# Query projection and product-key scores interleaved head by head, ahead of and between the first expert gathers

## The chip, the cores and the metric

The kernel runs on one core of one Trainium2 chip. The metric is the device time of one launch in microseconds (us); lower is better. The numbers of the kernel before are the median of three runs and one profiled execution.

## The reference, cut to what matters

The program is a two-block transformer on 256 tokens of width 1024, all in float32. The change lies in the first block's product-key expert layer (PEER): queries for 8 heads of 256 columns, each half scored against 128 sub-keys, the best 16 of the 16 x 16 sums chosen, and for each token and head 16 expert rows of `u` and of `v` fetched from a table in HBM.

```python
q = (x @ w_query)                      # 8 heads x 2 halves x 128
s = jnp.einsum('thpd,hpkd->thpk', q, subkeys)
sv, si = lax.top_k(s, 16)
cand = sv[..., 0, :, None] + sv[..., 1, None, :]
top_s, pos = lax.top_k(cand.reshape(..., 256), 16)
gate = softmax(top_s)
act = gelu(einsum('thkd,td->thk', u_tab[expert], x))
out = einsum('thk,thkd->td', gate * act, v_tab[expert])
```

## The kernel before, in words

**Engines and jobs.** The five engines run hand-written streams joined by semaphores. Each PSUM bank use is a job of the list `PLAN` (L34); job j uses bank j modulo 8, TensorE (PE) counts finished jobs in `pe_done`, and whoever copies a bank out counts `evac_done`, in the order of the list.

**Weights.** Query weights come in eight pieces of 1 MB, one for each head (pieces 0 to 7). ScalarE (ACT) casts a piece to a rounded float32r part (`split`, the "hi" part, L433), VectorE (DVE) or GpSimd (POOL) subtracts to get the "lo" part (`split_lo`, L440; L588), and PE forms the product with three matmuls per chunk (L2063 to L2065). Pieces 0 to 3 have raw, hi and lo slots 0 to 3 of their own. Pieces 4 to 7 use hi and lo slots 2, 3, 2, 3, so their cast waits until PE has used the piece two before. Their raw data (`QUERY_RAW`, L390) goes to: piece 4 a part of `PROJ`; piece 5 `SCR[:, 0:2048]`, where the sub-keys lay; piece 6 and 7 the hi and lo slot of piece 1, so that SP loads them only when PE has used piece 1 (L509 to L511).

**Queries and scores.** PE computes `queries(1)`, the rest of head 0, `queries(2)`, a part of the scores of head 0, then `queries(3)` to `(7)`, and then all scores in seven jobs of four matmuls (L2305 to L2333). Transposed queries of all heads lie in `qT`, all of `A`. ACT copies them there (`query_cols`, L921) and the scores into `SCORE` (L981).

**Expert rows.** A unit is one head for one 128-token half: 16 units in all. A unit has 16 gathers (POOL, L637) of one 1 MB buffer each (128 tokens x 2048 floats, `u` and `v` rows together), 256 in all, into 16 buffers `pair_buf` (L294). For each buffer DVE takes the dot product of the `u` part with the token (L1645), ACT makes gelu, the weight and a diagonal matrix for each block of four (L938, L943, L952), and PE sums the `v` part with it: eight matmuls for each block (`sum_rows`, L2347), then `rows_summed` is counted up and POOL may refill the four buffers. One full-float32 matmul stands as two instructions in the rows.

**The first unit.** Its buffers still hold weights, so `first_pairs` (L647) waits before the gathers: 0 to 3 (raw slots) for the splits of pieces 0 to 3, 4 and 5 (hi and lo slot 0) for the use of piece 0, 6 and 7 for the splits of pieces 6 and 7, 8 (`SCR`) for the split of piece 5, 9 and 10 (hi and lo slot 2) for the use of piece 6, 11 and 12 (slot 3) for the use of piece 7, 13 and 14 (`A`) and 15 (`B`, the sub-keys) for the last scores. POOL issues in program order, so whatever stands behind a waiting gather waits with it; the gathers of unit 1 follow (`pairs`, L663), each block of four when PE has summed the block of unit 0 (`rows_summed`), and when DVE has the indices of the unit (`idx_ready`).

**Route stages.** DVE's top-k of one unit is 17 small stages (L1567 to L1624); the gather indices are ready at stage 13.

Of the kernel before, what the change touches and what calls it, by code (L numbers as in the profile page):

```python
# [14 lines left out]
P = 128  # L15
# [65 lines left out]
def query_job(m):  # L81

    return J[f"query_{m}"] if m < 3 else J["query_rest"] + m - 3


def score_job(m):

    return J["score"] if m == 0 else J["score_rest"] + m - 1
# [52 lines left out]
def build(nc, a, out, at):  # L141
    ctx = ExitStack()
    with ctx:
# [123 lines left out]
        qT = A[:, :].rearrange("p (u t) -> p u t", u=16)  # L267
        SKN = SCR[:, 0:2048].rearrange("p (u n) -> p u n", u=16)
        SKT = B[:, 0:2048].rearrange("p (u n) -> p u n", u=16)
        SCORE = PROJ[:, 0:4096]  # L270
        N2W = PROJ[:, 4096:5120]
# [115 lines left out]
        class Piece:  # L387
# [3 lines left out]
                     RING + 3: ROWS[:, 5 * HALF:6 * HALF], RING + 4: ROWS[:, 9 * HALF:10 * HALF]}  # L391
        pieces, holder, raw_holder, uses, dmas = {}, [None] * 5, [None] * 9, [0] * 5, [0] * 9
        for name, n, h, src in PIECES:
# [5 lines left out]
            if r > RING:  # L399
                w.raw = QUERY_RAW[r]  # L400
            uses[h] += 1
# [53 lines left out]
        def _(sp):  # L455
# [50 lines left out]
            load("query", 4)  # L506
            sp.wait_ge(pe_done, END["subk_rest"])
            load("query", 5)
            sp.wait_ge(*pieces["query", 1].used)  # L509
            for n in range(6, 8):  # L510
                load("query", n)  # L511
# [68 lines left out]
        def _(pool):  # L580
# [66 lines left out]
            def first_pairs():  # L647

                pool.wait_ge(sem("idx_ready"), 1)
                for n in range(TOPK):  # L650
                    if n < 4:
                        query_split(n)
                    elif n == 4:
                        pool.wait_ge(*pieces["query", 0].used)
                    elif n in (6, 7, 8):
                        query_split((6, 7, 5)[n - 6])
                    elif n in (9, 11):
                        pool.wait_ge(*pieces["query", 6 if n == 9 else 7].used)
                    elif n == 13:
                        pool.wait_ge(pe_done, END["score_rest"])  # L660
                    gather(pair_buf[n], a["peer_uv"], 0, n, pair_loaded[n])
# [68 lines left out]
        def _(act):  # L730
# [190 lines left out]
            def query_cols(m):  # L921
# [3 lines left out]
                if m == 0:  # L925
                    d, src = qT[:, 0:2, P:S], PS[:, j % 8, 2 * P:4 * P]
                else:
                    d, src = qT[:, 2 * m:2 * m + 2, :], PS[:, j % 8, :]
                act.copy(d, src.rearrange("p (c t) -> p c t", c=2)).then_inc(evac_done, 1)

# [35 lines left out]
            gate_exp(0)  # L966
            query_cols(1)
            query_cols(0)
            for n in range(4, 8):
                split("query", n)  # L970
                query_cols(n - 2)
            weights(0, 0, 0)
            diag(0, 0, wait=False)
            query_cols(6)
            gate_exp(1)
            query_cols(7)
            for m in range(1, 8):
                j = score_job(m)
                act.wait_ge(pe_done, j + 1)
                act.wait_ge(evac_done, j)  # L980
                act.copy(SCORE[:, m * BANK:(m + 1) * BANK], PS[:, j % 8, :]).then_inc(evac_done, 1)  # L981
# [216 lines left out]
        def _(v):  # L1198
# [352 lines left out]
            nc.vector.tensor_copy(qT[:, 0:2, 0:P], first[:, 2 * P:4 * P].rearrange("p (c t) -> p c t", c=2)).then_inc(sem("head_ready"), 1)  # L1551
# [121 lines left out]
            split_lo(v, "query", 3)  # L1673
            j = J["score"]
            v.wait_ge(evac_done, j)
            freed(nc.vector.tensor_copy(SCORE[:, 2 * P:BANK], bank(j)[:, 2 * P:]), j, wait=True)
            for n in range(4, 6):
                split_lo(v, "query", n)
            v.wait_ge(sem("tokens_scaled"), 1)
            first_dots(0)  # L1680
            for n in range(6, 8):
                split_lo(v, "query", n)
            route_stages(1, 1, range(14))
            first_dots(1)
            route_stages(1, 1, range(14, 17))
            for b in range(2, 4):
                first_dots(b)
            v.wait_ge(evac_done, END["score_rest"])
# [990 lines left out]
```

## Time and profile before

| | |
|---|---|
| median of 3 runs | 1542.4 us (1539.7 to 1542.81) |
| profiled execution, first to last instruction | 1536.3 us |
| mean granted TensorE clock | 0.973 |
| expert rows, software queue q0 | 268.45 MB, 42.1% of 16 engines' span |
| gathers | 256, about 168 us to 821 us of the span |

No time of its own stands for the profiled execution beside its span; the median of the runs lies 6.1 us above the span. In the slices of the profile each digit is a tenth of busy time in one fortieth of the span (38.4 us). GB/s is what all DMA engines of the core moved.

### The profile page before, as it was taken

What the parts mean: (1) busy time and instruction counts of PE and PEld (TensorE: products, weight loads), DVE (VectorE), ACT (ScalarE), POOL (GpSimd) and SP (SyncE); (2) the same over time, 40 slices, a digit from 0 to 9 for tenths busy, and PEclk for the clock granted to TensorE, in tenths of its full rate; (3) what the DMA queues carried; (4) which work ended last, traced back from release to release, by engine and by line L of the source; (5) the groups of instructions that cost most, each with busy time, mean ns of one, the idle gap of its engine ahead of it and who ended that gap; (6) DMA issues with size and microseconds to landing.
All of it is one profiled execution on the core that took longest, in us unless ns stands there. A gap on an engine that the chain in (4) does not pass through costs nothing.

```text
span 1536.3 us, 18265 instructions
## 1 busy us (share of the span) xinstructions
PE 1381.1 (90%) x6001; PEld 969.0 (63%) x6001; DVE 1029.5 (67%) x1917; ACT 710.5 (46%) x1377; POOL 568.9 (37%) x541
## 2 busy tenths in 40 slices
PE   7999998778777887777779999999999999999998
PEld 6887963323333333333336878788888778888887
DVE  4885787666666666666655548659863686498734
ACT  5545453222333332233324463477645655776534
POOL 3040454333333333333344422055433512364414
PEclk9999999998998999999899999999999999999999
DMA  9295699999999999999998510567665443476650
GB/s 315 91 179 189 247 385 422 421 421 422 422 421 422 420 423 422 421 422 422 422 421 312 192 48 13 165 184 203 191 216 194 158 140 92 134 207 195 214 188 28
DMA packets 180739, 414.99 MB, mean 270 GB/s; under 512 B 9178, under 2 KB 113218, under 8 KB 148418
## 3 DMA queue, kind: packets, MB, share of 16 engines
q0 software_dynamic: 37440, 268.45, 42.1%
q1 hardware_dynamic: 143090, 145.66, 30.9%
q8 instruction: 38, 0.62, 0.2%
q14 instruction: 27, 0.22, 0.0%
q10 hardware_dynamic: 144, 0.04, 0.0%
HBM read 409.93 MB, written 4.19 MB: 270 GB/s over the span
## 4 chain that ended last, share of the span: by engine, by line
PE 52%; DMA 23%; DVE 9%; ACT 6%; POOL 5%; issue 4%; ACTq 0%; POOLq 0%; DVEq 0%
DMA expert_rows<-in_peer_uv,route_idx 13%; PE ps L2522 10%; DMA work_b<-in_peer_uv,route_idx 9%; PE ps L2347 8%; PE ps L2063 8%; PE ps L2065 8%; PE ps L2064 8%; PE ps L2523 5%; POOL weights_lo L588 2%; POOL expert_rows L637 2%; ACT weights_hi L433 2%; DVE weights_lo L440 2%; PE ps L2028 1%; DVE expert_rows L1645 1%; POOL ple_proj_lo L588 1%
## 5 line engine op out<-in xcount | busy, mean ns | idle before, releaser
L1645 DVE CUSTOM_DVE_ANT_0 expert_rows<-expert_rows,ps 128x1024 f32<-128x1024 f32 x180 | 219.4, 1220 | 133.9 <-DMA expert_rows<-in_peer_uv,route_idx 132.0
L2347 PE MATMUL ps<-expert_rows,proj 128*128 128x512 f32 x512 | 248.6, 644 | 63.5 <-ACT proj L952 63.5
L637 POOL DMA_INDIRECT expert_rows<-in_peer_uv,route_idx x191 | 184.5, 966 | 288.9 <-PE ps L2347 218.9
L588 POOL TENSOR_TENSOR weights_lo<-weights_raw,weights_hi 128x512 fp32r<-128x512 f32 x116 | 153.4, 1356 | 352.2 <-ACT weights_hi L433 310.3
L433 ACT CAST weights_hi<-weights_raw 128x2048 fp32r<-128x2048 f32 x98 | 185.5, 1917 | 106.3 <-PE ps L2065 82.6
L2347 PEld LDWEIGHTS ps<-expert_rows,proj 128*128 128x128 f32 x512 | 102.9, 206 | 208.4 <-issue 122.5
L2522 PE MATMUL ps<-x_normT,weights_hi 128*128 128x512 f32 x640 | 222.5, 393 | 0.0
L440 DVE TENSOR_TENSOR weights_lo<-weights_raw,weights_hi 128x2048 fp32r<-128x2048 f32 x69 | 163.1, 2370 | 61.2 <-ACT weights_hi L433 60.8
L938 ACT ACTIVATE proj<-proj 128x4 f32<-128x4 f32 x64 | 13.1, 205 | 408.0 <-DVE proj L1645 408.0
L2063 PE MATMUL ps<-weights_hi,x_normT 128*128 128x512 f32 (+1 forms) x496 | 188.2, 379 | 9.3 <-DVE weights_lo L440 3.2
L2065 PE MATMUL ps<-weights_hi,x_normT 128*128 128x512 f32 (+1 forms) x496 | 184.7, 372 | 0.0
L2064 PE MATMUL ps<-weights_lo,x_normT 128*128 128x512 f32 (+1 forms) x496 | 184.6, 372 | 0.0
L2523 PE MATMUL ps<-x_normT,weights_lo 128*128 128x256 f32 x640 | 178.3, 279 | 0.0
L2347 PE MATMUL ps<-expert_rows,scratch 128*128 128x512 f32 x252 | 120.8, 625 | 27.2 <-ACT scratch L952 27.2
L2522 PEld LDWEIGHTS ps<-x_normT,weights_hi 128*128 128x128 f32 x640 | 119.9, 187 | 27.1
L2523 PEld LDWEIGHTS ps<-x_normT,weights_lo 128*128 128x128 f32 x640 | 120.5, 188 | 0.0
L2063 PEld LDWEIGHTS ps<-weights_hi,x_normT 128*128 128x128 f32 x496 | 93.4, 188 | 30.3 <-issue 3.4
L2347 PEld LDWEIGHTS ps<-expert_rows,scratch 128*128 128x128 f32 x252 | 49.5, 201 | 97.8 <-issue 59.0
L2065 PEld LDWEIGHTS ps<-weights_hi,x_normT 128*128 128x128 f32 x496 | 93.4, 188 | 16.6
L2064 PEld LDWEIGHTS ps<-weights_lo,x_normT 128*128 128x128 f32 x496 | 93.5, 189 | 15.6 <-issue 0.2
L1875 DVE SCALAR_TENSOR_TENSOR work_a<-ps,conv_cols,work_a 128x254 f32<-128x254 f32 (+1 forms) x176 | 76.5, 475 | 29.3 <-ACT work_a L1088 25.1
L705 POOL TENSOR_TENSOR hidden_hi<-work_a 128x256 f32 (+1 forms) x44 | 41.8, 950 | 100.3 <-ACT work_a L1068 100.1
(369 smaller groups left out, 2411.3 us busy)
## 6 DMA issues: line engine op xcount, KB each, us to landing
weights_raw<-in_ffn_up SPq DMA_DIRECT2D x88, 512.0 KB, 5.0
weights_raw<-in_ffn_down SPq DMA_DIRECT2D x22, 1024.0 KB, 5.0
weights_raw<-in_ab_w_in SPq DMA_DIRECT2D x14, 1024.0 KB, 5.1
weights_raw<-in_w_in SPq DMA_DIRECT2D x12, 1024.0 KB, 7.9
weights_raw<-in_ple_gate SPq DMA_DIRECT2D x8, 1024.0 KB, 6.3
weights_raw<-in_c_w_in SPq DMA_DIRECT2D x6, 1024.0 KB, 5.7
weights_raw<-in_w_out SPq DMA_DIRECT2D x4, 1024.0 KB, 12.0
weights_raw<-in_peer_w_query SPq DMA_DIRECT2D x4, 1024.0 KB, 11.9
```

Source lines behind the costliest of these rows:

```text
L433: copy(w.hi[:, :], w.raw[:, :]).then_inc(hi_ready[w.h], 1)
L440: eng.tensor_tensor(w.lo[:, :], w.raw[:, :], w.hi[:, :].bitcast(F32), ALU.subtract).then_inc(lo_ready[w.h], 1)
L588: ins = pool.tensor_tensor(w.lo[:, c], w.raw[:, c], w.hi[:, c].bitcast(F32), ALU.subtract)
L637: nc.gpsimd.indirect_dma_start(out=dst, out_offset=None, in_=table, in_offset=bass.IndirectOffsetOnAxis(ap=r_idx[:, q, n:n + 1], axis=0)). ...
L1645: ins = nc.vector.tensor_tensor_reduce(out=rows, in0=rows, in1=tokens, scale=1.0, scalar=0.0, op0=ALU.mult, op1=ALU.add, accum_out=r_dot[: ...
L1875: ins = nc.vector.scalar_tensor_tensor(out=d, in0=PS[:, (j0 + 2 * q + g) % 8, 0:S - n], scalar=CONV[:, l, bass.ds(i * RING + (tap * 2 * FT ...
L2063: pe.matmul(o, x[0], w[0], start=first, stop=False)
L2064: pe.matmul(o, x[0], w[1], start=False, stop=False)
L2065: return pe.matmul(o, x[1], w[0], start=False, stop=last)
L2347: ins = pe.matmul(PS[:, (J[f"peer_{t}"] + m) % 8, :], DIAG[b][:, k, :], rows[:, m * BANK:(m + 1) * BANK], start=False, stop=False, skip_gr ...
L2522: pe.matmul(b.rearrange("p (a t) -> p a t", a=2), hi[:, c, g, :], x_both(c), start=c == 0, stop=False)
L2523: ins = pe.matmul(b[:, 0:S], lo[:, c, g, :], XHI[:, c, :], start=False, stop=c == KC - 1)
```

## The change

- `qT` is a ring of two heads in `SCR[:, 2048:3072]` (0.5 MB) in the place of all of `A`; the raw data of pieces 6 and 7 goes to the two halves of `A`, and the lo parts of pieces 5, 6 and 7 are written over their raw data.
- SP asks for pieces 4, 6 and 7 together behind the sub-keys, then for 5 once the sub-keys are used.
- The score jobs are now one for each head (both halves of tokens), each right behind the queries of the next head; `queries(7)` and the scores of heads 6 and 7 stand behind the first block of expert sums of unit 0.
- The first unit's gathers go in the order 0 to 7, 12, 10, 8, 9, 13, 11, 14, 15 with new waits.
- ACT's and DVE's work is put in a matching order.

```diff
-        ("query_1", 1), ("query_0", 1), ("query_2", 1), ("score", 1), ("query_rest", 5), ("score_rest", 7),
+        ("query_1", 1), ("query_0", 1), ("query_2", 1), ("score_1", 1), ("score_0", 1), ("query_3", 1), ("score_2", 1),
+        ("query_4", 1), ("score_3", 1), ("query_5", 1), ("score_4", 1), ("query_6", 1), ("score_5", 1), ("query_7", 1),
+        ("score_6", 1), ("score_7", 1),
...
-        qT = A[:, :].rearrange("p (u t) -> p u t", u=16)
+        qT = SCR[:, 2048:3072].rearrange("p (s q t) -> p s q t", s=2, q=2)
...
+        SCORE_HEADS = SCORE.rearrange("p (t n) -> p t n", t=TT)
...
-                     RING + 3: ROWS[:, 5 * HALF:6 * HALF], RING + 4: ROWS[:, 9 * HALF:10 * HALF]}
+                     RING + 3: A[:, 0:HALF], RING + 4: A[:, HALF:2 * HALF]}
+        QUERY_LO = {RING + 2: place("query_lo_5", [P, HALF], O_SCR, F32R),
+                    RING + 3: place("query_lo_6", [P, HALF], O_A, F32R),
+                    RING + 4: place("query_lo_7", [P, HALF], O_A + HALF, F32R)}
...
+                w.lo = QUERY_LO[r] if r in QUERY_LO else w.lo
...
-            load("query", 4)
+            for n in (4, 6, 7):
+                load("query", n)
             sp.wait_ge(pe_done, END["subk_rest"])
             load("query", 5)
-            sp.wait_ge(*pieces["query", 1].used)
-            for n in range(6, 8):
-                load("query", n)
...
-                for n in range(TOPK):
+                last_use = {4: 0, 12: 3, 10: 4, 8: 5, 9: 6, 11: 7}
+                for n in (0, 1, 2, 3, 4, 5, 6, 7, 12, 10, 8, 9, 13, 11, 14, 15):
                     if n < 4:
                         query_split(n)
-                    elif n == 4:
-                        pool.wait_ge(*pieces["query", 0].used)
-                    elif n in (6, 7, 8):
-                        query_split((6, 7, 5)[n - 6])
-                    elif n in (9, 11):
-                        pool.wait_ge(*pieces["query", 6 if n == 9 else 7].used)
-                    elif n == 13:
-                        pool.wait_ge(pe_done, END["score_rest"])
+                    elif n in last_use:
+                        pool.wait_ge(*pieces["query", last_use[n]].used)
+                    elif n == 15:
+                        pool.wait_ge(pe_done, END["score_7"])
                     gather(pair_buf[n], a["peer_uv"], 0, n, pair_loaded[n])
 
             def pairs(u, q, blocks=4):
...
+                    d, src = qT[:, m % 2], PS[:, j % 8, :]
...
+            def score_cols(m):
+                j = score_job(m)
+                act.wait_ge(pe_done, j + 1)
+                act.wait_ge(evac_done, j)
+                t0 = 0 if m else 1
+                act.copy(SCORE_HEADS[:, t0:TT, 2 * m * P:2 * (m + 1) * P],
+                         PS[:, j % 8, 2 * P * t0:].rearrange("p (t n) -> p t n", n=2 * P)).then_inc(evac_done, 1)
...
+            act.wait_ge(sem("bias_written"), 16)
             query_cols(1)
             query_cols(0)
-            for n in range(4, 8):
+            split("query", 4)
+            act.wait_ge(pe_done, END["score_0"])
+            query_cols(2)
+            act.wait_ge(lo_ready[pieces["query", 4].h], pieces["query", 4].count)
+            score_cols(1)
+            score_cols(0)
+            for n in (5, 6):
                 split("query", n)
                 query_cols(n - 2)
+                score_cols(n - 3)
             weights(0, 0, 0)
             diag(0, 0, wait=False)
-            query_cols(6)
+            split("query", 7)
+            for m in (5, 6):
+                query_cols(m)
+                score_cols(m - 1)
             gate_exp(1)
             query_cols(7)
-            for m in range(1, 8):
-                j = score_job(m)
-                act.wait_ge(pe_done, j + 1)
-                act.wait_ge(evac_done, j)
-                act.copy(SCORE[:, m * BANK:(m + 1) * BANK], PS[:, j % 8, :]).then_inc(evac_done, 1)
+            score_cols(6)
+            score_cols(7)
...
-            split_lo(v, "query", 3)
-            j = J["score"]
-            v.wait_ge(evac_done, j)
-            freed(nc.vector.tensor_copy(SCORE[:, 2 * P:BANK], bank(j)[:, 2 * P:]), j, wait=True)
-            for n in range(4, 6):
+            for n in (3, 4):
                 split_lo(v, "query", n)
+            v.wait_ge(evac_done, END["score_1"])
+            route_stages(1, 1, range(4))
+            split_lo(v, "query", 5)
             v.wait_ge(sem("tokens_scaled"), 1)
             first_dots(0)
-            for n in range(6, 8):
-                split_lo(v, "query", n)
-            route_stages(1, 1, range(14))
-            first_dots(1)
-            route_stages(1, 1, range(14, 17))
-            for b in range(2, 4):
+            split_lo(v, "query", 6)
+            route_stages(1, 1, range(4, 9))
+            split_lo(v, "query", 7)
+            route_stages(1, 1, range(9, 17))
+            for b in range(1, 4):
                 first_dots(b)
-            v.wait_ge(evac_done, END["score_rest"])
+            v.wait_ge(evac_done, END["score_7"])
...
-                t, h0 = m // 4, (m % 4) * 2
-                pe.wait_ge(evac_done, query_job(h0 + 1) + 1)
+                pe.wait_ge(evac_done, query_job(m) + 1)
                 b = bank(score_job(m))
-                for n in range(0 if m else 2, 4):
-                    u = 2 * h0 + n
-                    ins = pe.matmul(b[:, n * P:(n + 1) * P], qT[:, u, t * P:(t + 1) * P], SKT[:, u, :], start=True, stop=True)
+                for t in range(0 if m else 1, TT):
+                    for q in range(2):
+                        o = (2 * t + q) * P
+                        ins = pe.matmul(b[:, o:o + P], qT[:, m % 2, q, t * P:(t + 1) * P], SKT[:, 2 * m + q, :],
+                                        start=True, stop=True)
                 ins.then_inc(pe_done, 1)
 
             queries(1)
             head_columns(1, J["query_0"]).then_inc(pe_done, 1)
             queries(2)
+            scores(1)
             scores(0)
-            for m in range(3, 8):
+            for m in range(3, 7):
                 queries(m)
-            for m in range(1, 8):
-                scores(m)
-
-            def sum_rows(u, t, last=False):
-
-                for b in range(3 if last else 4):
+                scores(m - 1)
+
+            def sum_rows(u, t, last=False, blocks=range(4)):
+
+                for b in range(3) if last else blocks:
                     if last and b == 2:
                         for _ in range(4):
                             for acc in accs:
@@ -2352,8 +2369,13 @@
                 accs = [bank(J[f"peer_{t}"] + m) for m in range(2)]
                 for acc in accs:
                     pe.matmul(acc, zeros, C[:, 0:BANK], start=True, stop=False, skip_group_check=True)
-                for u in range(0 if t else 2):
-                    sum_rows(u, t)
+                if t == 0:
+                    sum_rows(0, 0, blocks=range(1))
+                    queries(7)
+                    scores(6)
+                    scores(7)
+                    sum_rows(0, 0, blocks=range(1, 4))
+                    sum_rows(1, 0)
```

## Rows read from the trace of the kernel before

**Rows 1.** The profile's slices: DMA busy tenths and GB/s, forty slices.

```profile
DMA  9295699999999999999998510567665443476650
GB/s 315 91 179 189 247 385 422 421 421 422 422 421 422 420 423 422 421 422 422 422 421 312 192 48 13 165 184 203 191 216 194 158 140 92 134 207 195 214 188 28
```

**Rows 2.** Busy time by stretch; columns: engines, granted clock, DMA share, GB/s.

```profile
166.00:190.00 24.00, 24.00 (x203) 24.00 (x202) 15.96 (x20) 8.12 (x8) 6.75 (x6) 1.00 0.90 350
190.00:200.00 10.00, 10.00 (x85) 10.00 (x85) 7.39 (x27) 7.76 (x14) 4.62 (x5) 1.00 0.61 208
200.00:210.00 10.00, 10.00 (x77) 8.80 (x76) 9.76 (x23) 6.24 (x11) 4.37 (x5) 1.00 1.00 410
210.00:217.00 7.00, 7.00 (x18) 3.17 (x17) 4.22 (x7) 4.61 (x18) 2.44 (x2) 1.00 1.00 420
400.00:600.00 200.00, 159.61 (x333) 65.85 (x333) 136.51 (x347) 60.58 (x195) 75.83 (x80) 0.93 1.01 422
```

**Rows 3.** POOL in order of time: start, length, what, idle before and releaser.

```profile
167.82 1.11 POOL L637 DMA_INDIRECT expert_rows<-in_peer_uv,route_idx  x1 [4.38 <-DVE route_idx L1611]
...
190.67 0.94 POOL L637 DMA_INDIRECT expert_rows<-in_peer_uv,route_idx  x1 [14.57 <-DVE weights_lo L440]
195.40 0.94 POOL L637 DMA_INDIRECT expert_rows<-in_peer_uv,route_idx  x1 [3.80 <-DVE weights_lo L440]
196.65 0.94 POOL L637 DMA_INDIRECT scratch<-in_peer_uv,route_idx  x1 [0.30 <-issue]
...
217.37 0.94 POOL L637 DMA_INDIRECT expert_rows<-in_peer_uv,route_idx  x1 [4.62 <-PE ps L2347]
```

**Rows 4.** PE in order of time: the score jobs, zero fill and sums.

```profile
172.36 0.61 PE L2323 MATMUL ps<-work_b,work_a 128*128 128x128 f32 x4
...
207.85 1.88 PE L2354 MATMUL ps<-consts 128*128 128x512 f32 x4
209.57 13.90 PE L2347 MATMUL ps<-expert_rows,proj 128*128 128x512 f32 x32
```

**Rows 5.** The chain that ended last, about 200 us: start, length, what.

```profile
201.76 6.27 PE ps L2323 x56
208.03 0.26 issue
208.28 0.94 POOL work_a L637
```

**Rows 6.** ACT in order of time.

```profile
184.57 1.91 ACT L433 CAST weights_hi<-expert_rows 128x2048 fp32r<-128x2048 f32 x1 [3.38 <-PE ps L2065]
...
190.33 1.90 ACT L433 CAST weights_hi<-expert_rows 128x2048 fp32r<-128x2048 f32 x1 [3.37 <-PE ps L2065]
192.14 0.58 ACT L929 COPY work_a<-ps 128x512 f32<-128x512 f32 x1
192.73 1.28 ACT L938 ACT_TABLE_LOAD   x1
194.03 0.21 ACT L938 ACTIVATE proj<-proj 128x4 f32<-128x4 f32 x1
194.32 0.85 ACT L943 ACTIVATE proj<-proj 128x1 f32<-128x1 f32 x4
195.21 1.28 ACT L952 ACTIVATE proj<-consts,proj 128x128 f32<-128x128 f32 x4
```

**Rows 7.** DVE in order of time: a split, a dot, the last dot of unit 0.

```profile
192.33 2.29 DVE L440 TENSOR_TENSOR weights_lo<-expert_rows,weights_hi 128x2048 fp32r<-128x2048 f32 x1 [2.44 <-ACT weights_hi L433]
...
223.21 1.23 DVE L1645 CUSTOM_DVE_ANT_0 work_b<-work_b,x_norm 128x1024 f32<-128x1024 f32 x1 [1.25 <-DMA work_b<-in_peer_uv,route_idx]
```

**Rows 8.** SP in order of time: query pieces 4, 5, then 6 and 7.

```profile
134.28 6.07 SPq L465 DMA_DIRECT2D proj<-in_peer_w_query  x1
157.41 0.37 SPq L465 DMA_DIRECT2D scratch<-in_peer_w_query  x1
166.57 0.99 SPq L465 DMA_DIRECT2D expert_rows<-in_peer_w_query  x2
```

**Rows 9.** Busy time by stretch, columns as rows 2.

```profile
130.00:146.00 16.00, 16.00 (x76) 13.32 (x76) 5.02 (x8) 5.21 (x16) 0.00 (x0) 1.00 0.95 295
146.00:150.00 4.00, 4.00 (x21) 3.28 (x20) 3.36 (x7) 4.00 (x4) 0.02 (x1) 1.00 0.01 5
150.00:157.00 7.00, 6.36 (x52) 5.73 (x51) 4.25 (x13) 5.90 (x17) 7.00 (x5) 1.00 0.00 0
```

**Rows 10.** Half-microsecond stretches round the lone gather, columns as rows 2.

```profile
191.50:192.00 0.50, 0.50 (x7) 0.50 (x6) 0.00 (x0) 0.50 (x1) 0.10 (x1) 1.00 0.00 0
192.00:192.50 0.50, 0.50 (x7) 0.50 (x6) 0.17 (x1) 0.50 (x2) 0.00 (x0) 1.00 0.99 197
...
195.50:196.00 0.50, 0.50 (x7) 0.50 (x6) 0.50 (x5) 0.50 (x3) 0.50 (x1) 1.00 0.21 66
```

**Rows 11.** The clock after a wait of PE: stretches, columns as rows 2.

```profile
236.00:240.00 4.00, 1.20 (x3) 0.19 (x1) 4.00 (x10) 2.14 (x9) 1.92 (x3) 0.97 1.01 422
240.00:244.00 4.00, 3.76 (x6) 1.73 (x7) 3.04 (x7) 0.19 (x1) 1.84 (x2) 0.61 1.01 420
```

More of the change, by code:

```diff
@@ L81, in query_job @@
 def query_job(m):
-    return J[f"query_{m}"] if m < 3 else J["query_rest"] + m - 3
+    return J[f"query_{m}"]
 def score_job(m):
-    return J["score"] if m == 0 else J["score_rest"] + m - 1
+    return J[f"score_{m}"]
 def shape_constants():
@@ L925, in query_cols @@
                 if m == 0:
-                    d, src = qT[:, 0:2, P:S], PS[:, j % 8, 2 * P:4 * P]
+                    d, src = qT[:, 0, :, P:S], PS[:, j % 8, 2 * P:4 * P]
                 else:
-                    d, src = qT[:, 2 * m:2 * m + 2, :], PS[:, j % 8, :]
+                    d, src = qT[:, m % 2], PS[:, j % 8, :]
                 act.copy(d, src.rearrange("p (c t) -> p c t", c=2)).then_inc(evac_done, 1)
+            def score_cols(m):
[5 more added lines that the diff above has]
+                         PS[:, j % 8, 2 * P * t0:].rearrange("p (t n) -> p t n", n=2 * P)).then_inc(evac_done, 1)
             def gate_exp(u):
@@ L1550, in _ @@
             v.wait_ge(sem("head_turned"), 1)
-            nc.vector.tensor_copy(qT[:, 0:2, 0:P], first[:, 2 * P:4 * P].rearrange("p (c t) -> p c t", c=2)).then_inc(sem("head_ready"), 1)
+            nc.vector.tensor_copy(qT[:, 0, :, 0:P], first[:, 2 * P:4 * P].rearrange("p (c t) -> p c t", c=2)).then_inc(sem("head_ready"), 1)
             norm_lo(1, 1)
@@ L2298, in _ @@
             for u in range(2):
-                ins = pe.matmul(b[:, u * P:(u + 1) * P], qT[:, u, 0:P], SKT[:, u, :], start=True, stop=True)
+                ins = pe.matmul(b[:, u * P:(u + 1) * P], qT[:, 0, u, 0:P], SKT[:, u, :], start=True, stop=True)
             ins.then_inc(pe_done, 1)
```

## The prediction

> **What bounds the kernel here.** I read the slices first: from about 190 us to 820 us DMA moves 420 to 424 GB/s in nearly every slice, and before that it has holes [rows 1]. That is the expert stage. In stretches, 400 to 600 us shows a DMA share of 1.01 while PE is busy 160 of 200 us and DVE 137 [rows 2]: the stage is a stream of 256 gathers of 1.049 MB, and at 422 GB/s one costs g = 1.049 MB / 422 GB/s = 2.485 us. Whatever leaves DMA idle between the first gather (167.82 us [rows 3]) and the last moves the end of the stream one for one, and the rest of the kernel behind it. So the question is only when the 16 gathers of unit 0 are done by DMA, and whether the stream stays full after that.
>
> Where is DMA not full before? 166 to 190 us runs at 350 GB/s on average, which includes 2.1 MB of query pieces 6 and 7, asked for at 166.57 us [rows 2, 8]; 190 to 200 us moves 208 GB/s [rows 2]. The cause stands in POOL's rows: gather 6 waits 14.57 us for a lo split and goes out at 190.67, gather 7 waits again and goes at 195.40, then 8 and the others follow 1.25 us apart [rows 3], faster than DMA takes them. From 200 us DMA is full (410, then 420 GB/s [rows 2]). So two things are to be had: the 2.1 MB in the stream (5.0 us) and the holes round 190 and 196 us.
>
> **PE's stream** is the clock of everything that frees a buffer. ACT's casts of pieces 6 and 7 start when PE is through with pieces 4 and 5, at 184.57 and 190.33: one query piece costs PE 5.76 us [rows 6]. A score job of four matmuls (eight instructions) costs 8 x 6.27/56 = 0.90 us, and POOL's gather 13 goes 0.26 us behind the last [rows 5]. The zero fill costs 209.57 - 207.85 = 1.72 us, one block of sums 13.90/2 = 6.95 us [rows 4].
>
> **Part 1: pieces 6 and 7 loaded early.** DMA is full to 146 us (295 GB/s on average) and empty to 157 us [rows 9]. Two more MB behind piece 4 (asked at 134.28) take 2.1 MB / 295 GB/s = 7.1 us, to about 153 us, ahead of piece 5's request at 157.41 [rows 8]. They stand behind the sub-keys on SP, and SP's long issue (6.07 us for piece 4) delays nothing else, as its next order is piece 5. Cost 0; without that empty stretch it would be the 5.0 us again. The stream loses 5.0 us of foreign bytes. The wait of ACT for the bias table is for a transfer long landed; cost 0.
>
> **Part 2: the order on PE up to query 6.** queries(2) end at 172.36 [rows 4]. Then scores 1 and 0 (0.90 + 0.45) to 173.7, and four times queries and scores (5.76 + 0.90), heads 3 to 6: pieces 3, 4, 5, 6 end at 179.5, 186.1, 192.8, 199.4, and scores 5 at 200.35. This needs the splits in time. Cast 1.90, copy 0.58 [rows 6], lo split 2.29 [rows 7]: lo 4 is ready at about 176.8 (wanted 180.4), lo 5 at 183.9 (wanted 187.0), lo 6 at 190.9, behind four dots of DVE (wanted 193.7), lo 7 at 197.3 (wanted 209.0). Every margin is over 2.7 us, so PE shouldn't wait, and the other edits of ACT and DVE (eight score copies for seven, the route stages of unit 1, done at about 200 us and wanted at 218.7) cost nothing; the cover is PE's 5.76 us per piece. Scores of head m need the copy of queries m, which is 5 us old by then.
>
> **Part 3: POOL's new order.** Gathers 0 to 7 now need only pieces 0 and 1 and the splits of pieces 0 to 3, so all eight go out by about 178 us. Gather 12 goes at 179.7, 10 at 186.4, 8 at 193.0, 9 and 13 from 199.6 on. DMA needs 168.8 + 8g = 188.7 for the first eight, two more to 193.7: the hole of 190 us is closed, a short one stays round 198 us. Thirteen gathers are through at about 207 us. So far the change is ahead.
>
> **Part 4: queries(7) behind the first block of sums, the term that decides.** From 200.35: zero fill 1.72, block 0 of the sums 6.95 (its diagonal is ready at about 193, so no wait), to 209.0; queries(7) 5.76, to 214.8; score 6 to 215.7, score 7 to 216.6 us. Before, query 7 ended at 201.76 [rows 5]. Gather 11 waits for the use of piece 7 and so goes out at 214.8 + 0.25 = 215.0, 14 right behind, 15 at 217.5. Block 0 has been summed since 209.0, but unit 1's gathers into its four buffers stand in POOL's program behind 11, 14 and 15: they go at 218.7 to 223, while before they went at 217.37 [rows 3]. DMA is empty from 207 us to the restart. Behind the wait of POOL stands thus the whole stream.
>
> **The sum.** Compare two restarts after an empty DMA, since the delay L from issue to flow then drops out. Before: 9 gathers (7 to 15) from 195.40, done at 195.40 + L + 9g. After: 3 gathers (11, 14, 15) from 215.0, done at 215.0 + L + 3g. The difference is 19.6 - 6g = 19.6 - 14.9 = +4.7 us. The stretch 200 to 210 us ran at 410 instead of 422 GB/s [rows 2], which is 0.3 us that the new one needn't lose: +4.4 to +4.7, and I take **+4.5 us**. Unit 1 keeps the stream full behind it: seven gathers cover 17.4 us, to about 234.8; ACT comes to the weights of block 1 only after score copy 7 (217.4; table load 1.28, gelu 0.2, weights 0.85, diagonals 1.28 [rows 6]: 221.2), and block 1 of the sums ends at 228 to 230, in time by 2 to 4 us. The bounds of the unseen restart: a lone gather's bytes (issued 190.67) were all moved by 196.0 us, 5.3 us from issue [rows 3, 10]; with 2g more, gather 15 would be in SBUF at 215.0 + 5.3 + 5.0 = 225.3, against its dot's start at 223.21 before [rows 7]: +2.1 us. At the other end is the plain sum with query 7 one microsecond late, +5.7. I take the plain sum because the restart of 195.40 is the same kind of event as the new one and 4.5 lies nearer to it.
>
> The profiled span is 1536.3 us, the median of the runs 1542.4, 6.1 us above it; I carry the difference over to the median: 1542.4 + 4.5 = **1546.9 us**. A measurement of this kernel tells about 0.2%, 3.1 us, from no change.
>
> A rule of the Trainium skill bears on the restart. DMA: Bandwidth & Descriptors, section "Anatomy of one DMA — SWDGE (gpsimd) path", fits one DMA as 2.0 us plus its bytes at 436 GB/s; for a lone gather that is an estimate of 4.4 us, and with two more, gather 15 in SBUF at 224.2, 1.0 us behind the row of before. The trace agrees roughly on the lone gather (5.3 us from issue), not on the speed of the stream (422 GB/s).
>
> **Rivals.**
> - *The tail comes cheap* (no change that can be told): the 3 us between the last byte of gather 15 by the sum (195.40 + about 2.3 + 9g = 220.1) and its dot at 223.21 are a lag that a freshly restarted stream doesn't have, so the stream loses only 2.1 us, by the lone gather [rows 10]: 1544.5. Against it: the lag was there after the restart of 195.40 too.
> - *Query 7 isn't late* (faster). The place is PE's stretch between scores 5 and queries(7). If zero fill and block 0 cost PE next to nothing there, query 7 ends at 206.1, gather 15 goes at 208.8, thirteen gathers are just drained, and the 16th is done at 208.7 + 3g = 216.2, against 220.1: -3.9 us, 1538.5. Each microsecond of the end of query 7 is one of the result; the change is even at 210.3 and measurably faster below 207.2. Against it: the 32 instructions of two blocks took 13.90 us with no wait between them [rows 4], and only the order as written would have to be wrong.
> - *A second hole at block 1* (slower still). PE waits from 216.6 to 221.2 us for ACT. Before, a wait of PE in 236 to 240 us was followed by a granted clock of 0.61 of full speed, near the 1.2 GHz level for part of that stretch, in 240 to 244 us [rows 11]. At half speed block 1 takes 13.9 us, to 235.1; its gathers flow at about 238.3 instead of 234.8: +3.5 more, 1550.4. For it: the wait is longer than the one before (4.6 against about 3 us). Against it: that clock was low only for part of four microseconds, about 1.6 us lost.
> - *The change doesn't show*: something early (the first indices, SP) shifts by a microsecond or two and hides it: within 3 us of 1542.4.
>
> **Chances.** Forecast 0.54 and second hole 0.13 (slower by over 0.2%: 0.67). Cheap tail 0.16 and no show 0.07 (within: 0.23). Query 7 not late 0.10 (faster). The range takes the forecast with its bounds, the second hole, the cheap tail and most of the no-show: 1541.5 to 1550.5; what is left out is mostly the faster case.
>
> **What the changed profile would show.** Right: DMA at about 300 GB/s to 152 us; gather 6 at about 176 us with no wait; PE's query 7 ending near 214.8 with block 0 of the sums ahead of it; a POOL wait of some 13 us for PE ahead of gather 11 at about 215; DMA near nothing from 207 to 216.5 us and full from there; the end of the gathers and all behind it 4 to 5 us later. Wrong: a gather 11 before 210 us, DMA not empty there, or a lo split that PE waits for. A span unchanged in spite of a 9 us hole would say that the stage isn't bound by the stream.

## The result, and the profile after

The changed kernel is slower: median 1543.22 us (1542.38 to 1547.26, 20 runs) against 1540.09 us (1537.44 to 1544.76, 20 runs) for the kernel before; the ratio is 1.0025 (95% interval 1.0018 to 1.0032), that is 3.9 us (2.8 to 4.9). The ratio is an estimate from all runs and not the quotient of the medians, which are 3.1 us apart. The forecast difference was 4.5 us. The forecast time, 1546.9 us, lies 3.7 us above the measured one, and 2.3 of that is its base: the three runs of before had a median of 1542.4, the twenty have 1540.09. So it is the difference that is compared. All differences below are ratios on this scale, where before is 1540.1. The profiled span is 1541.3 us against 1536.3. One execution each of e5 and e8 below took over 1950 us at a granted clock of 0.65 and stands in no interval.

The slices of the changed kernel's profile answer to [rows 1]: the slices at 154 to 230 us move 266 and 260 GB/s in the place of 247 and 385.

```profile
DMA  9297669999999999999998500567665443476650
GB/s 316 90 185 235 266 260 423 421 421 422 422 422 422 421 422 422 422 421 422 421 421 331 198 28 33 164 171 211 191 219 184 159 139 100 129 208 194 215 190 28
```

Busy time by stretch of the changed kernel (columns as in [rows 2], to which it answers, and to [rows 9]): the first rows show the early loads, the later ones the stream.

```profile
146.00:152.00 6.00, 5.87 (x34) 4.91 (x33) 4.49 (x9) 5.40 (x9) 1.91 (x2) 1.00 1.00 318
152.00:157.00 5.00, 4.48 (x38) 4.08 (x37) 3.13 (x10) 4.52 (x13) 5.00 (x4) 1.00 0.03 10
166.00:190.00 24.00, 24.00 (x205) 24.00 (x204) 17.18 (x32) 10.74 (x13) 12.87 (x10) 1.00 0.85 336
190.00:200.00 10.00, 10.00 (x86) 10.00 (x86) 8.79 (x23) 6.32 (x14) 1.02 (x2) 1.00 0.85 352
200.00:210.00 10.00, 10.00 (x34) 5.22 (x34) 7.33 (x15) 2.35 (x4) 1.79 (x2) 1.00 0.59 210
210.00:217.00 7.00, 6.71 (x57) 6.51 (x55) 1.37 (x4) 1.43 (x3) 1.55 (x2) 1.00 0.05 11
```

Pieces 6 and 7 now fill 146 to 152 us. The hole of 190 us is gone (352 instead of 208 GB/s), and a larger one stands at 208 to 217 us: 11 GB/s from 210 us on, where before moved 420.

POOL in order of time, for [rows 3]:

```profile
186.62 1.71 POOL L642 DMA_INDIRECT expert_rows<-in_peer_uv,route_idx  x1 [5.09 <-PE ps L2081]
193.27 0.94 POOL L642 DMA_INDIRECT scratch<-in_peer_uv,route_idx  x1 [4.94 <-PE ps L2081]
199.91 0.94 POOL L642 DMA_INDIRECT expert_rows<-in_peer_uv,route_idx  x1 [5.71 <-PE ps L2081]
...
215.15 0.94 POOL L642 DMA_INDIRECT expert_rows<-in_peer_uv,route_idx  x1 [13.06 <-PE ps L2081]
...
230.95 0.94 POOL L642 DMA_INDIRECT expert_rows<-in_peer_uv,route_idx  x1 [5.93 <-PE ps L2364]
```

These are gathers 10, 8, 9 and 11 of unit 0, each released by the last matmul of a query piece (L2081), and the first of block 1 of unit 1. Gather 11 waits 13.06 us. Why PE is so late stands in the chain that ended last, for [rows 5]:

```profile
199.64 0.89 PE ps L2339 x8
200.53 1.72 PE ps L2371 x4
202.25 6.87 PE ps L2364 x16
...
214.87 1.85 PE ps L2339 x16
```

The scores of head 5, the zero fill and block 0 of the sums (16 instructions) stand between query 6 and query 7, and the scores of heads 6 and 7 begin at 214.87. The last dot of unit 0 on DVE, 223.21 in [rows 7], is at 226.75:

```profile
226.75 1.23 DVE L1663 CUSTOM_DVE_ANT_0 work_b<-work_b,x_norm 128x1024 f32<-128x1024 f32 x1 [1.21 <-DMA work_b<-in_peer_uv,route_idx]
```

How far the stream itself is behind can be read from the bytes moved up to a time when both streams are full. The two rows are of 166 to 300 us, the first of the kernel before, the second of the changed one:

```profile
166.00:300.00 134.00, 121.96 (x527) 75.81 (x526) 98.12 (x240) 50.97 (x128) 56.40 (x55) 0.96 0.96 392
```
```profile
166.00:300.00 134.00, 119.61 (x520) 74.85 (x518) 94.12 (x230) 49.86 (x125) 54.63 (x53) 0.95 0.89 360
```

The difference is 32 GB/s x 134 us = 4.29 MB, of which 2.10 MB are the two query pieces that are no longer in this stretch; the 2.19 MB of gathers left are 5.2 us at 422 GB/s, give or take the 0.3 us that the rounding of the two rows is worth. From there on both move 422 GB/s. The order to store the output is issued at 1519.72 us before and at 1524.70 us after, the same distance; but the changed kernel's second profiled execution (e11 below) issues it at 1526.58 us with the stream as far behind as in the first, so that this agreement is in part luck.

### The profile page after: what moved, and what is told of

The parts are those of the page before. It is cut to its first block, busy times and chain, and to the rows that moved or that the text cites. A ratio compares the mean times of both kernels' runs of the same rounds, so it can differ in the third digit from the quotient of the medians.

```text
span 1541.3 us, 18262 instructions
## 1 busy us (share of the span) xinstructions
PE 1384.4 (90%) x6001; PEld 969.5 (63%) x6001; DVE 1027.6 (67%) x1916; ACT 711.0 (46%) x1378; POOL 569.0 (37%) x541
## 4 chain that ended last, share of the span: by engine, by line
PE 54%; DMA 22%; DVE 8%; ACT 7%; POOL 5%; issue 4%; POOLq 0%; DVEq 0%; ACTq 0%; SPq 0%
DMA expert_rows<-in_peer_uv,route_idx 22%; PE ps L2364 10%; PE ps L2544 10%; PE ps L2079 8%; PE ps L2081 8%; PE ps L2080 8%; PE ps L2545 5%; POOL expert_rows L642 3%; POOL weights_lo L593 2%; ACT weights_hi L440 2%; DVE weights_lo L447 2%; ACT proj L962 1%; PE ps L2044 1%; DVE expert_rows L1663 1%; POOL ple_proj_lo L593 1%
## 5 line engine op out<-in xcount | busy, mean ns | idle before, releaser
L2081 PE MATMUL ps<-weights_hi,x_normT 128*128 128x512 f32 (+1 forms) x496 | 184.8, 373 | 0.0
L2081 PEld LDWEIGHTS ps<-weights_hi,x_normT 128*128 128x128 f32 x496 | 93.4, 188 | 16.6
```

Source lines behind the costliest of these rows:

```text
L2081: return pe.matmul(o, x[1], w[0], start=False, stop=last)
```

## The experiments

Eleven runs follow: nine edits of the changed kernel (e10 is e2 again), and the changed kernel itself once more (e11). They were taken in three batches on three chips, each with runs of before of its own: e1, e2, e3 and e5 (median of before 1539.82 us), e4, e6, e7 and e8 (1539.82), and e9, e10 and e11 (1541.48). The times are against before.

The column "by bytes" is a second measure that needs no comparison of spans. It takes the mean GB/s in the 200 us from a profile's own first gather, less the two query pieces (2.10 MB) where they are loaded late, and says how far the stream is behind that of before, at 422 GB/s. Before moves 405 GB/s there, the changed kernel 384: 394.5 - 384 = 10.5 GB/s x 200 us = 2.1 MB, 5.0 us. The rounding of a row is worth up to 0.25 us.

| run | what | measured, us against before (95%) | by bytes, us | expected |
|---|---|---|---|---|
| changed | | +3.9 (+2.8 to +4.9) | +5.0 | +4.5 |
| e1 | query 7 ahead of block 0 | -1.5 (-2.8 to -0.2) | -0.7 | -0.8 |
| e2 / e10 | unit 1's first gathers ahead of 11, 14, 15 | +5.1 (+3.1 to +7.1) / +3.4 (+1.5 to +5.2) | +3.6 / +4.0 | +2.3 / +2.3 to +3.5 |
| e3 | e2, and ACT's block 1 ahead of query 7 | +3.2 (+1.8 to +4.8) | +2.6 | within 0.5 of 0 |
| e9 | e3, PE kept busy in its wait | -0.3 (-2.3 to +1.7) | +2.6 | 3 under e3 |
| e4 | late loads | +4.0 (+2.6 to +5.4) | +4.7 | +3.9 |
| e8 | e1, late loads | -1.1 (-2.5 to +0.3) | -0.9 | as e1 |
| e5 | 3.4 us more PE work ahead of query 7 | +8.3 (+6.3 to +10.3) | +7.8 | +7.3 |
| e7 | changed, no zero fill | +1.7 (+0.3 to +3.1) | +2.6 | +2.2 |
| e6 | e1, no zero fill | -2.6 (-4.0 to -1.2) | -2.1 | -3 |
| e11 | the changed kernel again | +2.3 (+0.5 to +4.2) | +4.5 | +3.9 |

Outside the last batch the two measures agree within 1.5 us. In the last batch all three times lie below their bytes, by 0.6 to 2.9 us, so times are best compared inside a batch.

**e1: query 7 back ahead of the first block of sums.**

```diff
-            for m in range(3, 7):
+            for m in range(3, 8):
                 queries(m)
                 scores(m - 1)
+            scores(7)
...
-                    sum_rows(0, 0, blocks=range(1))
-                    queries(7)
-                    scores(6)
-                    scores(7)
-                    sum_rows(0, 0, blocks=range(1, 4))
+                    sum_rows(0, 0)
```

> The changed kernel with queries(7) and the scores of heads 6 and 7 put back ahead of the first block of expert sums. Theory (the stream restarts when query 7 ends, and the first buffers of unit 1 wait for block 0 of the sums): query 7 ends at about 206.2, gather 11 goes at 206.4 and 15 at 208.9, the 16 gathers are drained at about 216.4; block 0 is summed at 216.7, unit 1's gathers go at 217.0 and flow from 219.4, against 220.2 for the 17th gather before: 0.8 us faster than before, about 5 us faster than the changed kernel (1539.3 on the scale where before is 1540.1), with a new hole of about 3 us at 216 to 219 us. Rival (what the prediction's faster case priced, nothing late behind query 7): 3.9 us faster than before. Rival (the order on TensorE isn't the cause): the time stays that of the changed kernel, 3.9 us slower than before.

Measured 0.9990 (0.9982 to 0.9999), 1.5 us faster than before: the whole loss of the change, and a little more, is this order. POOL of e1, and two stretches of DMA:

```profile
206.55 1.02 POOL L642 DMA_INDIRECT expert_rows<-in_peer_uv,route_idx  x1 [4.47 <-PE ps L2081]
...
217.47 1.18 POOL L642 DMA_INDIRECT expert_rows<-in_peer_uv,route_idx  x1 [5.32 <-PE ps L2365]
```
```profile
216.00:218.00 2.00, 2.00 (x6) 0.94 (x5) 1.86 (x4) 0.85 (x3) 0.53 (x1) 1.00 0.37 152
218.00:220.00 2.00, 2.00 (x6) 0.80 (x6) 1.20 (x3) 0.00 (x0) 1.69 (x2) 1.00 0.48 78
```

Gather 11 goes 8.6 us earlier. But unit 1's first gather, at 217.47, waits 5.32 us for block 0 of the sums, and DMA moves 78 GB/s at 218 to 220 us. So the gain isn't 8.6 us, nor the 3.9 under before that the prediction's faster case gave: a new hole takes the rest.

**e5 and e7: the end of query 7 moved by a known amount.** e5 puts eight matmuls of zeros ahead of it, e7 takes the zero fill away (the first matmul of block 0 starts the accumulators).

```diff
                     sum_rows(0, 0, blocks=range(1))
+                    for _ in range(4):
+                        for acc in accs:
+                            pe.matmul(acc[:, 0:S], zeros, C[:, 0:S], start=False, stop=False, skip_group_check=True)
                     queries(7)
```

> The changed kernel with eight matmuls of zeros of 256 columns (0.43 us each by the zero fill's row, 3.4 us in all) between block 0 of the sums and queries(7). Theory (each microsecond of query 7's end is one of the result): 3.4 us slower than the changed kernel, 7.3 slower than before; gather 11 goes at 218.6. Rival (the lateness of query 7 is partly hidden behind another wait, such as that for block 1 of the sums): clearly less, under 1.7 us.

```diff
                 for acc in accs:
-                    pe.matmul(acc, zeros, C[:, 0:BANK], start=True, stop=False, skip_group_check=True)
+                    if t:
+                        pe.matmul(acc, zeros, C[:, 0:BANK], start=True, stop=False, skip_group_check=True)
...
-                    sum_rows(0, 0, blocks=range(1))
+                    sum_rows(0, 0, blocks=range(1), fresh=True)
...
-                                            rows[:, m * BANK:(m + 1) * BANK], start=False, stop=False, skip_group_check=True)
+                                            rows[:, m * BANK:(m + 1) * BANK], start=fresh and n == 0, stop=False, skip_group_check=True)
```

> The changed kernel without the zero fill of the two accumulators of the first token half; the first matmul of block 0 starts them instead. Queries(7) end 1.72 us earlier, at about 213.1. Theory (each microsecond of query 7's end is one of the result): 1.7 us faster than the changed kernel, 2.2 slower than before. Rival (partly hidden): under 0.8 us faster than the changed kernel.

e5: ratio 1.0054 (1.0041 to 1.0067), 4.4 us over the changed kernel for 3.4 us of work. e7: 1.0011 (1.0002 to 1.0020), 2.2 us under it for 1.72 us. Within their intervals, of one to two microseconds, both follow the end of query 7 one for one. Counted from the first gather, gather 11 goes 3.5 us later in e5 (169.32 to 220.00 against 167.93 to 215.15) and 1.7 us earlier in e7 (167.94 to 213.46).

**e6: both.** e1 without the zero fill, by the same edit.

> e1_q7_first without the zero fill, as in e7_no_zero_fill. Theory (in e1 the hole at 216 to 219 us is unit 1's wait for block 0 of the sums): block 0 is summed 1.72 us earlier, at about 215, its gathers flow from about 217.7 instead of 219.4: 1.7 us faster than e1, about 3 us faster than before. Rival (e1's order is bound by the draining of the 16 gathers): the same as e1.

Ratio 0.9983 (0.9974 to 0.9992): 2.6 us faster than before and 1.1 under e1, the fastest version of the study. Its first gather of unit 1 goes at 216.31, that is 47.86 us behind its own first gather (168.45), in e1 49.56 us behind (167.91 to 217.47): 1.7 us sooner, as expected. The intervals of e1 and e6 overlap, so that 1.1 is no more than in the right direction; by bytes it is 1.4.

**e4 and e8: what the early loads are worth.**

```diff
-            for n in (4, 6, 7):
-                load("query", n)
+            load("query", 4)
             sp.wait_ge(pe_done, END["subk_rest"])
             load("query", 5)
+            sp.wait_ge(*pieces["query", 1].used)
+            for n in range(6, 8):
+                load("query", n)
```

> The changed kernel with only the load order of before: pieces 6 and 7 are asked for when TensorE has used piece 1 (about 166.5 us), into the same halves of the work buffer as in the changed kernel. Theory (thirteen gathers are drained 9 us before query 7 lets the stream restart, so 5.0 us of foreign bytes ahead of them are absorbed by the holes): 0 against the changed kernel, within 1 us, that is 3.9 slower than before. Rival (foreign bytes in the stream cost their 5.0 us wherever they are): 5 us slower than the changed kernel, 8.9 slower than before.

> e1_q7_first (queries 7 ahead of block 0 of the sums) with the load order of before as in e4_late_loads. Theory: the 5.0 us of bytes fall into the holes of 198 to 202 and 208 us, the 16 gathers are drained at about 216.4 as in e1, and unit 1's gathers still wait for block 0 of the sums: within 1 us of e1, about 1.5 faster than before. Rival (this order has too little idle left to absorb them): 2 to 5 us slower than e1, 0.5 to 3.5 slower than before.

e4: 1.0026 (1.0017 to 1.0035), the same as the changed kernel. e8: 0.9993 (0.9984 to 1.0002), the same as e1 within the intervals. DMA of e4 and then of the changed kernel, same columns:

```profile
190.00:200.00 10.00, 10.00 (x87) 10.00 (x86) 8.62 (x23) 6.30 (x14) 1.31 (x2) 1.00 1.02 420
200.00:210.00 10.00, 10.00 (x35) 5.22 (x34) 7.50 (x16) 2.09 (x3) 1.50 (x2) 1.00 0.70 276
```
```profile
198.00:200.00 2.00, 2.00 (x19) 2.00 (x18) 1.90 (x5) 0.32 (x1) 0.09 (x1) 1.00 0.27 111
```

With the loads late, the stream is full to 200 us; with the loads early, the same bytes are saved and DMA waits for query 6 instead (111 GB/s at 198 to 200 us). In either order PE's next release sets the time, so the 2.1 MB are worth nothing in these two orders.

**e2, e10, e3: the program order of POOL and of ACT.** e2 issues unit 1's first four gathers, whose buffers are free at 209 us, ahead of gather 11; e10 is e2 again. e3 also lets ACT make block 1's diagonals before it waits for query 7.

```diff
                     gather(pair_buf[n], a["peer_uv"], 0, n, pair_loaded[n])
+                    if n == 13:
+                        hold("idx_ready", 2)
+                        hold("rows_summed", 1)
+                        for k in range(4):
+                            gather(pair_buf[k], a["peer_uv"], 1, k, pair_loaded[k])
...
-            pairs(1, 1)
+            pairs(1, 1, first=1)
```

> The changed kernel with one edit on GpSimd: the first four gathers of unit 1 are issued ahead of gathers 11, 14 and 15 of unit 0. Theory (the program order on GpSimd holds back buffers that are free since 209 us): they go at 209.3 and flow from 211.7, the hole of 207 to 217 us halves; but block 1 of the sums is still only done at about 230.7, so its gathers flow at 233.2, while 20 gathers are drained at 229.0: a new hole of 4 us, and the 21st gather flows 1.6 us earlier than in the changed kernel: 1.6 us faster than it, 2.3 slower than before. Rival (the hole at 207 us alone counts): 5.8 us faster than the changed kernel, 1.9 faster than before.

> The kernel of e2_unit1_ahead once more, since five runs put it at 5.1 us over before (3.1 to 7.1) while its profile has the stream of gathers 1.3 us ahead of the changed kernel's by 300 us. Theory: with more runs it lies at 2.3 us over before, or up to 3.5 with block 1 of the sums 0.3 us late as its profile shows. Rival (its early gathers cost something elsewhere): 5 us over before, slower than the changed kernel.

```diff
             gate_exp(1)
+            weights(0, 0, 1)
+            diag(0, 1, wait=False)
             query_cols(7)
             score_cols(6)
             score_cols(7)
-            for b in range(1, 4):
+            for b in range(2, 4):
```

> As e2_unit1_ahead, and ScalarE makes the weights and diagonals of block 1 ahead of the copy of queries 7, in the 12 us in which it waits for it. Theory: block 1 of the sums starts behind the scores at 216.7 instead of 221.2 and is done at 223.7, in time for its gathers; block 2 waits for gather 11, which now lands at about 226.6, and is done at 237.7, its gathers flow at 240.3 against 238.9: 4 us faster than the changed kernel or a little more, within 0.5 us of before. Rival (hole at 207 us alone): as e2, 5.8 faster than the changed kernel. Rival (ScalarE's order is of no weight): the same as e2.

e2 missed: 1.0033 (1.0020 to 1.0046) in five runs, 1.0022 (1.0010 to 1.0034) in twelve as e10, beside 1.0015 (1.0003 to 1.0027) for the changed kernel in the same batch. That it gives no 5.8 us is shown. The 1.6 us expected show by bytes alone, where both profiled executions are some 1 us ahead of the changed kernel's; the times don't show them. Its profile has both holes that the theory named; DMA of e2:

```profile
210.00:212.00 2.00, 2.00 (x19) 2.00 (x18) 2.00 (x4) 0.00 (x0) 1.15 (x2) 1.00 0.00 0
212.00:214.00 2.00, 2.00 (x19) 2.00 (x18) 0.02 (x2) 0.00 (x0) 1.70 (x2) 1.00 0.70 197
...
232.00:234.00 2.00, 2.00 (x6) 0.82 (x5) 1.75 (x5) 0.20 (x1) 1.32 (x2) 1.00 0.00 0
```

The stream restarts at 212 us and stops at 232 us for block 1. e3 missed as well: 1.0021 (1.0012 to 1.0031), 3.2 us over before. PE of e3 shows where:

```profile
218.63 7.03 PE L2371 MATMUL ps<-expert_rows,proj 128*128 128x512 f32 x16
232.83 3.78 PE L2371 MATMUL ps<-scratch 128*128 128x512 f32 x4 [7.17 <-ACT scratch L967]
236.40 8.13 PE L2371 MATMUL ps<-expert_rows,scratch 128*128 128x512 f32 x16
```
```profile
229.00:233.00 4.00, 0.17 (x1) 0.17 (x2) 3.89 (x7) 2.33 (x9) 1.84 (x2) 0.50 1.01 422
233.00:236.00 3.00, 3.00 (x4) 1.34 (x5) 2.70 (x5) 0.62 (x4) 0.00 (x0) 0.50 1.02 423
```

PE waits 7.17 us for block 2, and behind the wait the granted clock is 0.50, the 1.2 GHz level: four instructions take 3.78 us, where the same four take 1.98 us in e9 below, at full clock. The block took about 10.1 us.

**e9: e3 with that wait filled.**

```diff
-                    sum_rows(0, 0, blocks=range(1, 4))
+                    sum_rows(0, 0, blocks=range(1, 2))
+                    for _ in range(7):
+                        for acc in accs:
+                            pe.matmul(acc[:, 0:S], zeros, C[:, 0:S], start=False, stop=False, skip_group_check=True)
+                    sum_rows(0, 0, blocks=range(2, 4))
```

> e3_unit1_ahead_act (measured 3.2 us slower than before where 0.3 was expected) with fourteen matmuls of zeros (256 columns, 0.43 us each, 6.0 us) between blocks 1 and 2 of unit 0's sums, in TensorE's wait of 7.2 us for block 2's diagonals. Theory (e3's miss is the clock: behind that wait block 2 took 10.1 instead of 6.9 us, granted clock 0.50, and its gathers came 3 us late): block 2 takes about 7 us, its gathers go 3 us earlier than in e3 measured from the first gather: 3 us faster than e3, within 0.5 us of before. Rival (the miss comes from elsewhere, the clock costs nothing): the same as e3 or slower.

```profile
225.25 6.21 PE L2387 MATMUL ps<-consts 128*128 128x256 f32 x28
232.45 1.98 PE L2371 MATMUL ps<-scratch 128*128 128x512 f32 x4 [0.99 <-ACT scratch L967]
234.27 7.03 PE L2371 MATMUL ps<-expert_rows,scratch 128*128 128x512 f32 x16
```

Block 2 is back at about 7 us, and its gathers go 70.1 us behind the first gather instead of 73.1. So the clock did cost 3 us there. The ratio is 0.9998 (0.9985 to 1.0011), 3.5 us under e3, where 3 was expected. But e3 was measured in another batch, and by bytes e9's profiled execution gains nothing on e3's. The rows are of 200 us from the first gather, e3 first:

```profile
170.02:370.02 200.00, 170.57 (x615) 94.80 (x614) 138.25 (x339) 71.46 (x194) 79.95 (x81) 0.94 0.95 389
```
```profile
169.76:369.76 200.00, 174.58 (x644) 99.40 (x642) 137.98 (x338) 71.02 (x192) 79.49 (x81) 0.96 0.96 389
```

The 3 us are lost again at the first blocks of unit 1. PE is ready for them earlier in e9, but their diagonals are not, so it now waits there for ACT; PE of e3 and then of e9:

```profile
251.12 14.00 PE L2371 MATMUL ps<-expert_rows,proj 128*128 128x512 f32 x32 [1.43 <-ACT proj L967]
```
```profile
250.73 16.44 PE L2371 MATMUL ps<-expert_rows,proj 128*128 128x512 f32 x32 [4.29 <-ACT proj L967]
```

Behind the 4.29 us the clock was 0.50 (250 to 255 us), behind e3's 1.43 us it was 1.00. The two blocks took 16.44 instead of 14.00 us, the gathers that wait for the first of them go 91.35 us behind the first gather instead of 89.04, and DMA has a hole that e3 hasn't; DMA of e3 and then of e9:

```profile
262.00:268.00 6.00, 6.00 (x16) 2.65 (x15) 5.28 (x13) 1.10 (x4) 3.18 (x4) 1.00 1.01 422
```
```profile
262.00:268.00 6.00, 6.00 (x16) 2.65 (x15) 5.69 (x17) 1.50 (x8) 2.87 (x5) 1.00 0.85 288
```

So the clock is shown as the cause of the late block 2, not as the whole of e3's miss of about 3 us: with the wait filled, the next one gives the profiled execution the same distance. What the fill is worth in time stays open.

**e11: the control.**

> The changed kernel itself, as a control on the same chip: 3.9 us slower than before within its interval (2.8 to 4.9).

1.0015 (1.0003 to 1.0027): lower than the 1.0025 of the twenty runs, with the intervals overlapping. Its profile has gather 11 at 215.06 us and its stream 4.5 us behind, as in the first.

## Why the prediction was right, and where its steps were off

- **Parts 1 to 3 (loads, PE to query 6, POOL's order)** held to some tenths of a microsecond: gathers 10, 8 and 9 at 186.62, 193.27 and 199.91 us against 186.4, 193.0 and 199.6. The gathers before them were later than forecast, 6, 7 and 12 at 178.11, 179.35 and 180.59 us against about 176, 178 and 179.7, since the issue of gather 5 took 2.55 us on POOL where most take 0.94; DMA still had work then, so it cost nothing. No split was late. What they were worth was another matter: the prediction said that "two things are to be had", 5.0 us of foreign bytes among them. e4 and e8 show that these bytes are worth nothing where the next buffer is released by PE anyway. The sum wasn't touched, since it compares restarts and not bytes.
- **Part 4 (query 7)** is the cause. Gather 11 went at 215.15 us against 215.0 forecast. e1 takes the loss away, e5 and e7 move it with query 7.
- **The sum**: +4.5 forecast, about 5 by the bytes of the profiled pair, 3.9 in the runs. The term that was off in the profile is what a restart costs. The prediction took the delay L as equal, and took off 0.3 us that the stretch of 200 to 210 us had lost and the new one "needn't lose". But the new one lost as well:

```profile
214.00:224.00 10.00, 5.62 (x28) 3.88 (x27) 3.31 (x5) 7.35 (x22) 7.02 (x7) 0.76 0.69 247
```

These 2.47 MB are 5.9 us at 422 GB/s, so the effective start of the flow is 218.1 us, 3.0 us behind gather 11's issue: the new restart ran at 340 to 381 GB/s from 218 to 224 us. By the same reckoning the restart of 195.40 cost 2.5 us: 9.12 MB were moved from 190 to 217 us [rows 2], 8.07 without the lone gather, which is 19.1 us and gives a start at 197.9 us. So the term is +0.5 and not -0.3, and 215.15 - 195.40 - 14.9 + 0.5 = 5.3 us, as the bytes have it. The 3.9 of the runs lies about as far under the forecast as this lies over it; that single executions differ by more than this is shown below.
- **Rival "cheap tail"** (+2.1): its first half happened, its price didn't. Gather 15's bytes were through at 218.1 + 3g = 225.6 us and its dot started 1.2 us later; before, the same count gives 197.9 + 9g = 220.3 and 2.9 us. So the lag did shrink, and the dot starts only 3.5 us later. But the next gathers stand behind the bytes and not behind the dot, and the stream is some 5 us behind. The interval of the twenty runs (2.8 to 4.9) leaves 2.1 out; that of e11 alone (0.5 to 4.2) wouldn't. The fixed-cost rule of the Trainium skill (DMA: Bandwidth & Descriptors, section "Anatomy of one DMA — SWDGE (gpsimd) path") gave an estimate of 224.2 us for the landing of gather 15; the dot at 226.75 us doesn't agree.
- **Rival "query 7 isn't late"** was priced wrongly at -3.9 us. The step that failed is its last: with query 7 early nothing was thought to be late next. Block 0 is then summed only at about 216.7 us, and unit 1's gathers wait for it, going at 217.47 us where before had 217.37. So e1 gains 1.5 us on before and not 3.9.
- **Rival "second hole at block 1"**: its first half happened and its price didn't. Behind PE's wait of 4.38 us for ACT the clock was 0.50:

```profile
221.09 9.59 PE L2364 MATMUL ps<-expert_rows,proj 128*128 128x512 f32 x16 [4.38 <-ACT proj L962]
```
```profile
218.00:220.00 2.00, 0.00 (x0) 0.00 (x0) 0.00 (x0) 1.92 (x7) 1.50 (x2) 0.81 0.91 381
220.00:222.00 2.00, 0.91 (x1) 0.50 (x2) 1.31 (x3) 1.08 (x5) 1.58 (x2) 0.50 0.97 340
...
230.00:232.00 2.00, 2.00 (x6) 0.95 (x5) 1.90 (x13) 1.70 (x3) 0.94 (x1) 1.00 0.99 418
```

The clock was back at 0.98 in 226 to 228 us. Block 1 took 9.6 us instead of 6.95, not the 13.9 that the rival priced, and its gathers went at 230.95 us, later than the 228 to 230 forecast for its end, but DMA still had work to 235 us and shows no hole (418 GB/s at 230 to 232 us).

## What to carry to other kernels

Where one engine's stream releases the buffers of a DMA stream, the order on that engine is the plan: write down which buffers each piece of work frees and when, and check at every time that the next transfer in the issuing queue's own order is among the freed ones. Freeing four buffers early is worth nothing if the queue stands in front of a gather that needs another. And price every variant to its next late event: moving query 7 by 8.6 us gave 5.4 us of time, since another wait stood right behind, and in e9 the 3 us that block 2 won were lost at the next wait.

## What the runs showed that was not expected

- A wait of TensorE of a few microseconds costs more than itself. After waits of 4.4 and 7.2 us the granted clock was 0.50, and the next block of sums took 9.6 and 10.1 us instead of 6.95. Filling the second wait with 6.2 us of matmuls of zeros brought the block back to about 7 us, but the next wait, 4.3 us long, then had the same effect.
- The same program has a clock dip in some executions and not in others. e2 and e10 are the same kernel; the rows are their PE and clock at 108 to 112 us, long before the changed code:

```profile
108.00:112.00 4.00, 2.93 (x23) 2.52 (x23) 3.79 (x7) 1.02 (x3) 0.00 (x0) 1.00 0.93 140
```
```profile
108.00:112.00 4.00, 3.54 (x18) 3.51 (x18) 3.79 (x7) 0.47 (x3) 0.00 (x0) 0.60 0.94 194
```

With the dip (0.60, e10) the first gather went at 169.56 us, without it (e2) at 168.57, though e10 was 0.6 us ahead at 92 us: about 1.6 us in one execution. The profiled executions of e3, e5 and e9 have the dip too (0.57 to 0.61) and their first gathers at 169.3 to 170.0 us; the nine without it have them at 167.6 to 168.6. Another scatter comes late: the changed kernel's two profiled executions have their first gathers 0.1 us apart and their orders to store the output 1.9 us apart. Differences of single spans under two microseconds aren't evidence in this kernel; positions in the stream are better counted from the first gather.
